# Seven half products for eight in 17 pairs of a ConvFFN's up projection, with weight sums formed in HBM by GpSimd's DMAs

## The reference, cut to what matters

```python
def conv_ffn(x, prev, lp):          # d_model 1024, d_ff 2816
    h = rms_norm(x, ffn_pre)
    gate, val = h @ w_up[:, :2816], h @ w_up[:, 2816:]
    gate = causal conv of width 3 over tokens, with conv_b (prev holds the two rows before)
    return (gelu(gate) * val) @ w_down
```

## Time and profile before

| | |
|---|---|
| median of 3 runs | 2004.49 us (2001.93 to 2006.17) |
| the profiled execution | 2001.52 us, its span 1999.7 us |
| busy in the span | PE 97%, PEld 90%, DVE 62%, ACT 37%, POOL 2% |
| granted clock of TensorE | 0.987 of full speed |
| up projection of layer 0 | from about 605 us to 862 us of the span |
| up projection of layer 1 | some 990 us later |
| GpSimd's last rows of pair 0 | at 625 us in layer 0, at 1615 us in layer 1 |

### The profile page before, as it was taken

The page is one execution under the profiler, slowest core; times in us unless marked ns, Lnnn a source line. Parts: engine busy times, 40 slices in busy tenths (PEclk is TensorE's granted clock), DMA queues, the critical chain, the costliest instruction groups (busy, mean ns, idle before and its releaser), DMA issues.

```text
span 1999.7 us, 53466 instructions
## 1 busy us (share of the span) xinstructions
PE 1937.3 (97%) x22496; PEld 1799.3 (90%) x22496; DVE 1243.2 (62%) x2070; ACT 732.4 (37%) x1394; POOL 30.6 (2%) x143
## 2 busy tenths in 40 slices
PE   8999999999999999999999999999999999999997
PEld 7999898766799999999999998887677999999997
DVE  3475868888638665542355767688786476656323
ACT  3223345563634222232232233545626342222321
POOL 0000000000000000000000000000000000000000
PEclk9999999999999999999999998999999999999999
DMA  5225443244222332232332264333442222233222
GB/s 218 90 80 164 149 138 128 65 119 132 86 89 64 96 96 86 95 95 95 101 142 85 75 204 140 118 107 93 121 126 72 78 85 94 86 96 96 95 96 89
DMA packets 153010, 214.29 MB, mean 107 GB/s; under 512 B 18497, under 2 KB 118338, under 8 KB 151362
## 3 DMA queue, kind: packets, MB, share of 16 engines
q1 hardware_dynamic: 134050, 200.38, 31.9%
q10 hardware_dynamic: 18720, 10.49, 1.8%
HBM read 202.58 MB, written 16.59 MB: 110 GB/s over the span
## 4 chain that ended last, share of the span: by engine, by line
PE 78%; DVE 13%; ACT 3%; DMA 2%; issue 2%; ACTq 1%; SPq 0%; DVEq 0%
PE ps L925 18%; PE ps L927 18%; PE ps L926 18%; PE ps L1315 4%; PE ps L1193 1%; DMA ring<-in_w 1%; PE ps L1286 1%; PE ps L1182 1%; PE ps L946 1%; PE ps L947 1%; DVE arena L2194 1%; DVE arena L2156 1%; PE ps L1279 1%; PE ps L1195 1%; DVE arena L2203 1%
## 5 line engine op out<-in xcount | busy, mean ns | idle before, releaser
L927 PE MATMUL ps<-hm_hi,ring_lo 128*128 128x260 f32 x1568 | 444.9, 284 | 0.0
L1882 DVE TENSOR_TENSOR ring_lo<-ring,ring_hi 128x1024 fp32r<-128x1024 f32 x130 | 159.3, 1225 | 306.3 <-ACT ring_hi L1479 304.1
L927 PEld LDWEIGHTS ps<-hm_hi,ring_lo 128*128 128x128 f32 x1568 | 296.9, 189 | 0.0
L925 PE MATMUL ps<-hm_hi,ring_hi 128*128 128x260 f32 x1008 | 285.5, 283 | 0.0
L926 PE MATMUL ps<-hm_lo,ring_hi 128*128 128x260 f32 x1008 | 284.6, 282 | 0.0
L1479 ACT ACTIVATE ring_hi<-ring 128x1024 fp32r<-128x1024 f32 x130 | 137.8, 1060 | 323.0 <-DMA ring<-in_w 314.6
L927 PE MATMUL ps<-hf_hi,ring_lo 128*128 128x260 f32 x704 | 198.9, 283 | 0.0
L927 PE MATMUL ps<-in_hi,ring_lo 128*128 128x260 f32 x704 | 198.8, 282 | 0.0
L925 PEld LDWEIGHTS ps<-hm_hi,ring_hi 128*128 128x128 f32 x1008 | 189.6, 188 | 1.8 <-issue 1.8
L926 PEld LDWEIGHTS ps<-hm_lo,ring_hi 128*128 128x128 f32 x1008 | 189.7, 188 | 0.0
L1882 DVE TENSOR_TENSOR ring_lo<-ring,extra_hi 128x1024 fp32r<-128x1024 f32 x64 | 78.4, 1225 | 152.8 <-ACT extra_hi L1479 151.1
(11 more groups left out here) (453 smaller groups left out, 4578.4 us busy)
## 6 DMA issues: line engine op xcount, KB each, us to landing
ring<-in_w SPq DMA_DIRECT2D x200, 512.0 KB, 3.6
extra<-in_kv_cmp SPq DMA_DIRECT2D x96, 128.0 KB, 2.3
arena<-in_kv_cmp SPq DMA_DIRECT2D x80, 128.0 KB, 2.6
slot<-in_kv_cmp SPq DMA_DIRECT2D x80, 128.0 KB, 2.4
out_win_old<-in_win SPq DMA_DIRECT2D x16, 511.0 KB, 4.4
slot<-in_k_sel SPq DMA_DIRECT2D x72, 64.0 KB, 2.0
extra<-in_k_sel SPq DMA_DIRECT2D x72, 64.0 KB, 1.9
arena<-in_v_sel SPq DMA_DIRECT2D x72, 64.0 KB, 2.1
```

The lines of the kernel that those rows point to most:

```text
L925: mmul(out, wh, hi[:, k, cols], start=(k == 0), stop=False)
L927: last = mmul(out, wl, hi[:, k, cols], start=False, stop=(ci == len(chunks) - 1 and k == k1 - 1))
L1882: v.tensor_tensor(w_low(l, n), w_place(l, n), w_high(l, n), SUB).then_inc(S["w_lo"], 1)
```

## The change

Pairs 5 to 21 (`NG` = 17 of them) no longer run as two tiles. For a pair take the 2 x 2 blocks of the product: input channels in two halves of four `k` blocks, output channels gate and value, tokens in two halves. That is eight half products of 4 blocks x 3 matmuls = 12 matmuls each. The Winograd form of Strassen's method needs seven, of sums of blocks. So:

- **Weight sums.** Four combinations of the pair's quarter chunks (128 x 512) are put together in HBM in a new buffer `sums`, by DMAs from GpSimd's queue, 68 plain and 68 adding ones for each layer. They start in layer 0 when ten input tiles are out of PSUM, and in layer 1 when layer 0's last rows are copied. They come in four batches, each waited for by GpSimd, which only then goes on to the last rows.
- **Token sums.** DVE forms four sums of halves of the scaled activations (`twins`, after `scaled` on ACT), ACT and DVE split them (`twin_high`, `twin_low`), while pairs 2 to 4 run.
- **Loads.** SP loads four pieces A, Z, V and F for each pair (3.5 chunks' worth where it was 2), each into its own double buffer; the first Z, V and F only after all sums are in.
- **The products.** `product` runs them in the order s2, a12, s3, s1, a11 of the next pair, a22, s4. Partial sums are shared by ACT copying a PSUM bank into another (`seed` b and c), on which PE goes on adding, and into SBUF (`seed` p7 and u4), from which DVE forms the value halves (`val_first`, `val_second`). The gate half tiles come straight from PSUM.
- **Elsewhere.** The first tap of the convolution goes to ACT (`tap`). `EARLY` is 4 now, since the room is taken. The first three down chunks are split during the last pair, and PE waits for the last pair's value halves before the down projection. Several semaphores of the input phase are merged into one for each engine (`side_pe`, `side_act`, `side_dve`), at the same points.

```diff
+PAIRS = 5
+NG = FT - PAIRS
+HK = KB // 2
...
+def seven_order():
+
+    out = [(0, "a11")]
+    for g in range(NG):
+        out += [(g, "s2"), (g, "a12"), (g, "s3"), (g, "s1")] + ([(g + 1, "a11")] if g + 1 < NG else []) + [(g, "a22"), (g, "s4")]
+    return out
...
-        EARLY = (HS - 14272) // TOK
+        EARLY = PAIRS - 1
...
+                    if n == C_UP + 2 * PAIRS - 1:
+                        sp.wait_ge(S["q_sum"], 16 * SUM_DMAS * (l + 1))
+                        for pair in "ZVF":
+                            pair_load(pair, 0)
+                        for g in range(1, NG):
+                            for pair in "AZVF":
+                                pair_load(pair, g)
...
+                def product(q):
...
+                    pe.wait_ge(S["q_lo"], SPLIT_COUNT * l + TWINS + PREPARED_AT[PAIR[name], g])
...
+                    elif name == "s2":
+                        pe.wait_ge(S["q_seed"], SEEDS * l + 4 * g + 1)
...
+                    for k in range(HK):
+                        w = slice(k * P, (k + 1) * P)
+                        new = name in ("a11", "s3") and k == 0
+                        mmul(out, wh[:, w], hi[:, k, :], start=new, stop=False, skip_group_check=True)
+                        mmul(out, wh[:, w], lo[:, k, :], start=False, stop=False, skip_group_check=True)
+                        last = mmul(out, wl[:, w], hi[:, k, :], start=False, stop=(k == HK - 1), skip_group_check=True)
+                    last.then_inc(S["q_pe"], 1)
...
+                pe.wait_ge(S["q_gate"], 2 * NG * (l + 1) - 1)
+                pe.wait_ge(S["q_val"], 2 * NG * (l + 1))
...
+                    A(dst, src, ACT.Copy, scale=-1.0 if kind in ("b", "u4") else 1.0).then_inc(S["q_seed"], 1)
...
+                act.wait_ge(S["q_pe"], SEVENS * (l + 1))
+                act.wait_ge(S["q_val"], 2 * NG * (l + 1))
...
+                if l == 0:
+                    pool.wait_ge(S["evac_v"], NT)
+                else:
+                    pool.wait_ge(SL[l - 1]["ffn_t"], FT * l)
+                for first in (True, False):
+                    for n in range(NG):
+                        for i, src in (((0, val_a), (1, gate_a), (2, val_a), (3, gate_b)) if first else ((0, val_b), (2, gate_a))):
+                            to = w_sums[l, n, :, 512 * i:512 * (i + 1)]
+                            if first:
+                                pool.dma_start(to, part(n, *src)).then_inc(S["q_sum"], 16)
+                            else:
+                                pool.dma_start(to, part(n, *src), accum_op=ALU.add).then_inc(S["q_sum"], 16)
+                            done += 1
+                    pool.wait_ge(S["q_sum"], 16 * (SUM_DMAS * l + done))
...
+                    if i == 2:
+                        conv_sample()
+                        twins()
+                    if i in (3, 4):
+                        twin_low(2 * i - 6)
+                        twin_low(2 * i - 5)
...
+                    else:
+                        split_w(C_DOWN, C_DOWN + 1, C_DOWN + 2)
+                    val_second(g)
```

More of the change, by code:

```diff
@@ L70, with roped_at, prepared @@
 KEEP = 5
+PAIRS = 5
[6 more added lines that the diff above has]
+    return out
+SEVEN = seven_order()
+SEVEN_AT = {key: i + 1 for i, key in enumerate(SEVEN)}
+SEVENS = len(SEVEN)
+SEEDS = 4 * NG
+TWINS = 5
+SIDE_PE = {"gate": 1, "rope": 1, "vt": 9, "cmpp": 9}
+SIDE_ACT = {"gate_sg": 1, "gate_ev": 2, "staged": 3, "vt": 4, "cmpp_p": 5, "cmpp_t": 6, "kcp": 7}
+SIDE_DVE = {"staged": 2, "ready": 9, "cmpp_x": 10, "cmpp_h": 11}
+def roped_at(r):
+    return r if r == 1 else r + 1
+PAIR = {"a11": "A", "a12": "A", "s1": "Z", "s2": "Z", "s3": "V", "a22": "V", "s4": "F"}
+LAST = {"A": "a12", "Z": "s1", "V": "a22", "F": "s4"}
+def prepared():
+    out = [("A", 0), ("Z", 0), ("V", 0)]
+    for g in range(NG):
+        out += ([("A", g + 1)] if g + 1 < NG else []) + [("F", g)] + ([("Z", g + 1), ("V", g + 1)] if g + 1 < NG else [])
+    return out
+PREPARED_AT = {key: i + 1 for i, key in enumerate(prepared())}
+SPLIT_COUNT = TWINS + len(PREPARED_AT)
+SUM_DMAS = 8 * NG
 COLS = {}
@@ L690, in build @@
         x_ok = [ctx.enter_context(nc.semaphore(f"x_ok{k}")) for k in range(KB)]
+        quarters_in = {pair: x_ok[2 * i:2 * i + 2] for i, pair in enumerate("AZVF")}
+        w_sums = I["sums"]
         const_ok = ctx.enter_context(nc.semaphore("const_ok"))
@@ new lines, in scaled, with twin_high @@
+                def scaled():
+                    act.wait_ge(S["kv_stored"], 16 * (l + 1))
+                    for k in range(KB):
+                        ins = A(xg[:, k, :], x[:, k, :], ACT.Copy, scale=C("ffn_pre", k))
+                        o.go(ins)
+                    o.tell(S["q_hi"])
+                def twin_high(i):
+                    act.wait_ge(S["q_twin"], l + 1)
+                    A(t_hi[:, i, :, :], tf[:, i, :, :], ACT.Copy, scale=1.0 if i else -1.0).then_inc(S["q_hi"], 1)
@@ L1835, in _ @@
                     o.tell(S["ffn_t"])
+                for i in range(FT):
+                    last_rows(i)
         @block.vector
@@ L2414, in _, with low, gate_half @@
                 norm_out(3)
-                for i in range(FT):
+                def low(pair, g):
+                    dve.wait_ge(S["q_hi"], SPLIT_COUNT * l + TWINS + PREPARED_AT[pair, g])
+                    full, lo = full_pair(l, g, pair)
+                    v.tensor_tensor(lo, full, high_pair(g, pair), SUB).then_inc(S["q_lo"], 1)
+                def gate_half(g, h):
+                    i = PAIRS + g
+                    letter, product = ("a", "a12") if h == 0 else ("c", "s4")
+                    dve.wait_ge(S["ffn_t"], FT * l + i - 1)
+                    dve.wait_ge(S["ffn_c"], FT * l + i - 1)
+                    dve.wait_ge(S["q_pe"], SEVENS * l + SEVEN_AT[g, product])
+                    v.tensor_tensor(gx[:, i % 2, 2 + h * HALF:2 + (h + 1) * HALF], ps[:, seven_bank(g, letter), 0:HALF], rstd[:, h, :], MUL).then_inc(S["q_gate"], 1)
@@ new lines, in twins @@
+                def twins():
+                    dve.wait_ge(S["q_hi"], SPLIT_COUNT * l + 1)
+                    first, second = xg[:, 0:HK, :], xg[:, HK:KB, :]
+                    o.do(v.tensor_tensor(tf[:, 0, :, :], first[:, :, 0:HALF], first[:, :, HALF:TOK], ADD))
+                    o.go(v.tensor_tensor(tf[:, 1, :, :], tf[:, 0, :, :], second[:, :, HALF:TOK], SUB))
+                    o.do(v.tensor_tensor(tf[:, 2, :, :], second[:, :, HALF:TOK], first[:, :, HALF:TOK], SUB))
+                    o.go(v.tensor_tensor(tf[:, 3, :, :], second[:, :, 0:HALF], tf[:, 1, :, :], SUB))
+                    o.tell(S["q_twin"])
@@ L2416, in _, with twin_low @@
+                def twin_low(i):
+                    dve.wait_ge(S["q_hi"], SPLIT_COUNT * l + i + 2)
+                    o.go(v.scalar_tensor_tensor(t_lo[:, i, :, :], tf[:, i, :, :], 1.0 if i else -1.0, t_hi[:, i, :, :], MUL, SUB))
+                    o.tell(S["q_lo"])
+                for i in range(PAIRS):
                     if 2 * i >= FRONT:
-                        split_w(*(C_UP + c for c in next_chunks(2 * i)))
+                        split_w(*up_chunks(2 * i))
                     n = n_dense[0]
```

375 lines of the change are left out of this document (313 added, 62 removed).

## The result

The changed kernel takes **2022.23 us** (median of 5 runs, 2012.41 to 2025.38); the kernel before took 2004.49 on the same chip. The ratio is 1.0077, with a 95% interval of 1.0048 to 1.0106: 0.8% slower, where 0.8% faster was forecast. The profiled execution took 2025.38 us, its span is 2023.2.

A forecast was written before the change was run, and what follows sets the result against it. PE was taken to bound the kernel (busy 1937.3 of 1999.7 us). 48.8 us of removed matmuls less 34.4 of joins left 14.4, giving 1987.1 from the profiled run or 1990.1 from the median; forecast 1989, range 1968 to 2032.

The forecast's parts named there:

- Removed matmuls, 48.8 us: Up projection: 408 matmuls fewer over 17 pairs and 2 layers, at 0.1197 us each, save 48.8 us.
- The middle: Up projection's steady loop: PE keeps its own pace, 10.05 us a round; DVE needs 9.0 and ACT 6.7.
- The sums are in time: GpSimd's weight-sum DMAs in HBM finish before its last rows; upper bound 490 us, still 74 us early.
- At no cost on the path: Weight-sum traffic during the earlier stages: 170 us of all engines, 0.64 of 564 us free, so no time added.
- in time, but in the way: Rival: while the sums run, weight and page loads share engines, losing 6 to 16 us: 1995 to 2005; chance 0.12.
- The six joins: Six places around the up projection's loop where PE waits for late work: 17.2 us a layer, 34.4 in all.
- The sum: Whole kernel: 48.8 us saved less 34.4 us of joins leaves a gain of 14.4 us.
- the middle is not PE's: Rival: DVE or ACT takes over 10.05 us a loop round; with 11.0 the time is 2021; chance 0.14.
- the sums are late: Rival: sum DMAs take 4.15 us or more each and delay GpSimd's last rows: 2023 to 2285; chance 0.16.
- signs of being wrong: PE standing in the middle for DVE's or ACT's results, GpSimd's pair 0 rows late, or the mixing half growing.
- Issuing from GpSimd: Sum DMAs prepared only while DVE rests: 1.18 us for each of 136, anything above makes them late, 2023 or more.

The follow-up runs named there:

- experiment 1: The changed kernel without GpSimd's 272 sum DMAs, SP loading pieces of the weights in their place: 1998.05 us, ratio 0.9989.
- experiment 2: The kernel before, with the same 272 sum DMAs from GpSimd added and their results unused: 2031.49 us, ratio 1.0166.
- experiment 7: The changed kernel, sums included, with another order of DVE's and ACT's work at both joins: 1990.41 us, ratio 0.9951.
- experiment 10: Also the narrow kernel: changed kernel with reordered joins and no sums, plus GpSimd's 272 DMAs 32 columns wide for 512: 1958.21 us, ratio 0.9799.
- second measurement: The changed kernel measured once more, unaltered, against the kernel before: 2026.28 us, ratio 1.0126.
- Experiment 3: The changed kernel with all 272 GpSimd DMAs as plain copies, none adding: 2025.48 us, ratio 1.0134.
- the new joins: The changed kernel with DVE's and ACT's work reordered at both joins: 1990.41 us with sums, 1977.48 with at most two sum DMAs in flight, 1958.83 without sums.

## Why the prediction was wrong

- **Removed matmuls, 48.8 us**: right. 408 fewer, at 0.1195 us each.
- **The middle**: right. PE never waits there; DVE took 8.0 us of the 10.05, where the sum had 9.0.
- **The sums are in time**: right, and by more than was said (459 us; 639 allowed). Each landed later than the 2.8 and 4.4 us counted (medians of 6.3 and 6.7), but several were in flight at once.
- **"At no cost on the path": this step failed.** It was argued from room: 170 us of all engines, 0.64 of 564 us free. Experiments 1, 2 and 7 show 18 to 33 us in its place, and experiment 10 that it goes with the bytes. The room was real, since the sums finished early. But a load that PE needs is not served from an average: while the sums flowed, weight chunks landed after 6.3 us for 3.5 and 128 KB pages after 4.1 for 2.3. The rival "in time, but in the way" had this mechanism, at 6 to 16 us and a chance of 0.12. It took the slack ahead of a use (some 4 us) as cover; ACT's waits of 6.8 to 8.5 us, for at most 2.6 from 80 to 165 us before, show that it was not enough. Its price left out the clock: in the changed kernel 14.4 of 27.2 us are matmuls that ran slower, in experiment 2 it is 7.7 of 28.8 (PE busy 1945.0 us there, 1937.3 before).
- **The six joins**: each place right, the waits 14.4 us in layer 0 and 13.7 in layer 1 for 17.2. **The term was mis-sized**, since a wait was priced at its own length. Behind the longer ones the clock is at half: experiment 1 puts the joins at 46.6 us for 34.4. Taking waits of 25.6 us away gave 39.2, and the trace shows 11.9 of it as the same matmuls running faster.
- **The sum**, by the first measurement of the changed kernel: 48.8 - 46.6 - 17.6 = -15.4 us, against a forecast of +14.4. The mis-sized joins took 12.2 of it, the sums' traffic 17.6. Without the traffic the change would still have gained only 2.2 us; with the joins forecast right, the traffic alone would have turned 14.4 into a loss of 3. By the second measurement the traffic took 27.4.
- **Luck**: the rivals "the middle is not PE's" and "the sums are late" gave 2021 and 2023, and 2022 was measured, but neither occurred: PE never waited in the middle, and the sums were 182 us early. The range up to 2032 rested on them. What did occur is what the prediction named as signs of being wrong, pair 0's rows late and a longer mixing half.
- **Issuing from GpSimd**: the case, weighed in the prediction, in which GpSimd is shut out whenever DVE runs did not occur. In the narrow kernel, from 75 to 165 us, GpSimd was busy with 84 issues for 48.5 us and DVE for 61.6 of the same 90, so at least 20 us of issuing ran beside DVE's work. By the Trainium skill (SBUF — State Buffer, "SBUF: two separate sides") issuing takes a port that DVE shares; no run here shows a cost of it. Experiment 10 issued all 272 and has a ratio of 0.9799, for 0.9795 without any.

What stays open: which part of the way the bytes fill. Experiment 3 shows that it is not the engines' busy share by itself, since 12.2% cost as much as 19.1%; nothing here tells HBM from the engines' queues. The half clock is shown to come with the waits and to go with them, and not by what rule.

## What to carry to other kernels

A transfer "in the background" is to be priced by the loads that share its stretch: read their landing times in those stretches (6.3 us for 3.5 here), not the free share or the median over the whole. The DMA share alone does not tell: with narrow DMAs it stood at 0.81 and 0.91 in two stretches of 10 us (180 to 190, 210 to 220), and nothing was lost. If it must run, a few in flight over the whole time that there is cost less here than bursts (11 us of 31, with the new joins; in the changed kernel itself the gain was within the noise), and the profiles show that gain in layer 1 only. And a wait of PE of several us costs its length and about half as much again through the clock (25.6 us of waits were worth 39.2), so joins between two ways of working deserve as much care as the loop: here they took 46.6 us of 48.8, and another order of the same work on DVE and ACT gave back 39.

## What was not expected of the hardware

- GpSimd issues plain DMAs in runs of seven (0.53 us each), then stands for some 6 to 9 us "on issue"; the records of adding ones are 1.08 us long and overlap (57.0 us busy for 68), in runs of one to three. With narrow DMAs the standing falls from 169.9 to 66.0 us for the same 136.
- After a 4.5 us wait the granted clock was 0.51 over ten us; 36 matmuls ran there for 86, two of the ten us being the end of the wait.
- A 128-partition copy of two columns on GpSimd, 0.19 us before, takes 0.82 us on average in the changed kernel. The sums' DMAs are not the reason: without them (experiment 1) it is 0.82 as well.
